# Another order of the query tiles in stick-breaking attention, on Trainium2

## The reference, cut to what matters

```python
z = jnp.einsum('bhqd,bhkd->bhqk', qi, kf).astype(jnp.float32) * scale
qpos = bi * SB_BLOCK + jnp.arange(SB_BLOCK)
before = kpos[None, :] < qpos[:, None]
log_beta = jax.nn.log_sigmoid(z)
log_1m = jnp.where(before, jax.nn.log_sigmoid(-z), 0.0)
tail = lax.cumsum(log_1m, axis=3, reverse=True) - log_1m
w = jnp.where(before, jnp.exp(log_beta + tail), 0.0)
return jnp.einsum('bhqk,bhkd->bhqd', w.astype(vf.dtype), vf)
...
mixed = jnp.concatenate(
    [rms_norm(o_a, ga), rms_norm(o_b, gb), rms_norm(o_c, gc)], axis=-1)
y = jnp.einsum('bse,ed->bsd', mixed, w_out[l])
```

## Time and profile before

| | |
|---|---|
| median of 3 runs | 1045.97 us (1045.08 to 1047.18) |
| profiled execution | 1044.86 us |
| its span | 1043.1 us |
| TensorE busy | 1015.7 us, 97% of the span |
| VectorE, ScalarE, GpSimd busy | 795.8, 572.3, 90.5 us |
| granted TensorE clock, mean | 0.998 |

### The profile page before, as it was taken

One profiled execution on the slowest core, in us unless ns is written; L12 is line 12 of the kernel. 1 busy time (PEld: TensorE's weight loads), 2 busy tenths in 40 slices (PEclk: granted clock), 3 DMA queues, 4 the chain that ended last, 5 costly groups with the idle time before them and its releaser, 6 DMA issues.

```text
span 1043.1 us, 12464 instructions
## 1 busy us (share of the span) xinstructions
PE 1015.7 (97%) x4982; PEld 820.1 (79%) x4982; DVE 795.8 (76%) x740; ACT 572.3 (55%) x753; POOL 90.5 (9%) x71
## 2 busy tenths in 40 slices
PE   8999999998989999999999999999999999999996
PEld 6878778786757787788788888788888788888784
DVE  6247659688578579877878867998776998777998
ACT  6513432658767536677653567333657333666454
POOL 0014113021211143000000000000000000000000
PEclk9999999999999999999999999999999999999999
DMA  9421111200011544013013022022031031035004
GB/s 327 139 76 41 41 41 41 71 11 2 2 41 41 193 165 167 1 42 120 1 47 116 1 76 87 1 79 83 1 121 41 1 121 41 1 123 201 1 0 161
DMA packets 38657, 74.65 MB, mean 72 GB/s; under 512 B 3236, under 2 KB 12744, under 8 KB 38600
## 3 DMA queue, kind: packets, MB, share of 16 engines
q1 hardware_dynamic: 38600, 73.86, 20.5%
HBM read 65.46 MB, written 8.39 MB: 71 GB/s over the span
## 4 chain that ended last, share of the span: by engine, by line
PE 87%; DVE 5%; ACT 4%; issue 1%; DMA 1%; SPq 1%; ACTq 0%; DVEq 0%
PE ps L720 27%; PE ps L724 27%; PE ps L722 26%; PE ps L889 2%; PE ps L935 2%; PE ps L793 1%; PE ps L960 1%; DMA xt<-in_x_turned 1%; ACT work L1158 1%; DVE out_gained L2090 1%; DVE y L2148 1%; DVE y L2039 1%; ACT sb_w L1330 1%; PE ps L824 1%; ACT sb_r L1326 0%
## 5 line engine op out<-in xcount | busy, mean ns | idle before, releaser
L720 PE MATMUL ps<-a_op,b_op 128*128 128x512 f32 x448 | 175.6, 392 | 3.0 <-ACT ut L1435 1.1
L720 PE MATMUL ps<-b_op,a_op 128*128 128x512 f32 x448 | 174.7, 390 | 3.9 <-issue 3.9
L724 PE MATMUL ps<-a_op,b_op 128*128 128x512 f32 x448 | 174.5, 389 | 0.0
L724 PE MATMUL ps<-b_op,a_op 128*128 128x512 f32 x448 | 174.4, 389 | 0.0
L722 PE MATMUL ps<-a_op,b_op 128*128 128x512 f32 x448 | 174.4, 389 | 0.0
L722 PE MATMUL ps<-b_op,a_op 128*128 128x512 f32 x448 | 174.4, 389 | 0.0
L1484 ACT CAST a_op<-f 128x1024 fp32r<-128x1024 f32 x56 | 58.8, 1050 | 113.2 <-PE ps L724 73.0
L720 PE MATMUL ps<-act_hi,w_hi 128*128 128x512 f32 x288 | 114.5, 398 | 2.6 <-issue 1.3
L1996 DVE TENSOR_TENSOR b_op<-wq,b_op 128x1024 fp32r<-128x1024 f32 x96 | 117.0, 1219 | 0.0
L724 PE MATMUL ps<-act_hi,w_lo 128*128 128x512 f32 x288 | 112.2, 390 | 0.0
L722 PE MATMUL ps<-act_lo,w_hi 128*128 128x512 f32 x288 | 112.2, 390 | 0.0
(11 more groups left out here) (224 smaller groups left out, 1682.9 us busy)
## 6 DMA issues: line engine op xcount, KB each, us to landing
wq<-in_w_ff_in SPq DMA_DIRECT2D x16, 1024.0 KB, 5.6
wq<-in_w_ff_out SPq DMA_DIRECT2D x16, 1024.0 KB, 5.2
stage<-in_w_in SPq DMA_DIRECT2D x16, 512.0 KB, 4.8
y<-in_x SPq DMA_DIRECT2D x4, 1024.0 KB, 12.5
stage<-in_w_out SPq DMA_DIRECT2D x8, 512.0 KB, 3.9
h_spill<-y SPq DMA_DIRECT2D x8, 512.0 KB, 2.7
h_back<-h_spill SPq DMA_DIRECT2D x2, 2048.0 KB, 11.9
out<-y SPq DMA_DIRECT2D x8, 512.0 KB, 2.8
```

The lines of the kernel that those rows point to most:

```text
L720: nc.tensor.matmul(dst, stat[0], mov[0], start=first, stop=False, skip_group_check=chained)
L724: return nc.tensor.matmul(dst, stat[1], mov[0], start=False, stop=last, skip_group_check=chained)
```

## The change

The units come in another order: the first pair runs t = 7, 6, 5, 4, 0, 1, 2, 3, the second 4, 5, 6, 7, 3, 2, 1, 0. The fill rows move with them and again leave out the units with one and two key blocks (now u = 4, 5, 14, 15). SUM_UNIT goes from 6 to 4, and with it GpSimd's addition of the window squares (from ahead of the mask of head 10 to ahead of that of head 6), TensorE's partition sums and VectorE's reading of them, which is now tied to head 12. The window group's roundings on ScalarE go from heads 17 and 19 to 9 and 11, their VectorE halves from heads 21 and 23 to 13 and 15. The squares after heads 3 and 5 and the splits after heads 7 and 21 stay. The table load goes from behind head 29's copies to behind the loop.

```diff
--- before.py
+++ after.py
@@ -392,7 +392,9 @@
 
 
 
-        UNITS = [(p, t) for p in range(2) for t in reversed(range(TOK))]
+
+        UNITS = [(p, t) for p, ts in ((0, (7, 6, 5, 4, 0, 1, 2, 3)), (1, (4, 5, 6, 7, 3, 2, 1, 0)))
+                 for t in ts]
         HEADS = 2 * len(UNITS)
         CHAIN = 4
         LEAD = 3
@@ -421,10 +423,11 @@
 
 
         WINDOW_ROWS = 2
-        FILL_UNITS = (0, 1, 2, 3, 4, 5, 8, 9, 10, 11, 12, 13)
+        FILL_UNITS = (0, 1, 2, 3, 6, 7, 8, 9, 10, 11, 12, 13)
         N_EARLY = WINDOW_ROWS + len(FILL_UNITS)
-        SUM_UNIT, SPLIT_HEADS = 6, (7, 21)
-        MIX_HEADS = (17, 19)
+        SUM_UNIT, SPLIT_HEADS = 4, (7, 21)
+        AFTER_SUMS = min(u for u in FILL_UNITS if u > SUM_UNIT)
+        MIX_HEADS = (9, 11)
 
         def row_of(u):
             return WINDOW_ROWS + FILL_UNITS.index(u)
@@ -976,7 +979,7 @@
                     pe.wait_ge(turned_copied, 4)
                 elif n < N_EARLY:
                     pe.wait_ge(row_copied, n)
-                    if n == row_of(FILL_UNITS[6]):
+                    if n == row_of(AFTER_SUMS):
                         pe.wait_ge(grp_var, 2)
                 elif n == N_EARLY:
                     pe.wait_ge(row_copied, N_EARLY)
@@ -1015,7 +1018,7 @@
                 if u in FILL_UNITS:
                     recurrent_out(row_of(u), range(2, OUT_K))
                 if u == SUM_UNIT:
-                    pe.wait_ge(row_copied, row_of(FILL_UNITS[6]))
+                    pe.wait_ge(row_copied, row_of(AFTER_SUMS))
                     group_sums(1, 7, win_sq[:, 0, :])
             weighted(len(UNITS) - 1)
             for n in range(N_EARLY, 2 * TOK):
@@ -1394,8 +1397,7 @@
                     split_hi(N_IN + 1, (N_IN + 1) % 2)
                 if n == SPLIT_HEADS[1]:
                     split_hi(N_IN + 2, N_IN % 2)
-                if n + LEAD == HEADS:
-                    nc.scalar.preload_act_table_set("natural_log_exp_and_others")
+            nc.scalar.preload_act_table_set("natural_log_exp_and_others")
             output_copy(len(UNITS) // CHAIN - 1)
             group_rsqrt(1)
 
@@ -1914,7 +1916,7 @@
                     split_lo(N_IN + 1, (N_IN + 1) % 2)
                 if n == SPLIT_HEADS[1] + 2:
                     split_lo(N_IN + 2, N_IN % 2)
-                if a and u == SUM_UNIT + 1:
+                if n == 2 * SUM_UNIT + 4:
                     group_variance(1, 7)
             left = list(range(N_EARLY, 2 * TOK))
             for k in range(2):
```

## The result

The changed kernel takes 1050.26 us (median of six runs, 1049.93 to 1051.42) against 1045.97 (1045.08 to 1047.18): a ratio of 1.0040, 95% interval 1.0030 to 1.0051. It is slower by 4.3 us, by more than the 0.2% that can be told from no change, and inside the range of 1045.8 to 1050.4, though 2.3 above the forecast of 1048.0. Its profiled execution took 1050.91 us with a span of 1049.2.

The account below looks back on a forecast made before the run. TensorE, computing for 97% of the span, was taken as the bound. Idle time rising from 3.8 to 6.3 us, less 0.45 for the table load, gave +2.0 on the median 1045.97: 1048.0, range 1045.8 to 1050.4.

Parts of the forecast that it names:

- the old handover: Kernel before, 297 to 308 us: smallest unit of first pair to largest of second; 2.81 us TensorE idle, forecast to go.
- Part 1: Window sum ahead of head 6's mask on GpSimd: TensorE idle 4.2 us before head 6's transposes, 4.05 as shown.
- Part 2: Weight split after head 7 beside one-block units: 1.2 us idle at unit 6's scores, replacing 0.75 before.
- Part 3: Roundings beside units 4 and 5 without fill: waits of 0.55 at unit 7's scores, 0.9 at unit 5's weighted sum.
- Part 4: From unit 6 on: heads ready 2 to 6 us early; the waits of 2.81 and 0.21 us go.
- Part 5: Table load behind the loop: TensorE goes on sooner after head 31's copy, gain 0.45 us, bound 0.2 to 0.5.
- The sum: Whole kernel: idle time 3.8 to 6.3 us, less 0.45 at the end: +2.0 us, bounds +0.8 and +3.2.
- The clock falls: Rival: TensorE drops to half clock after the 4.2 us wait; 4 us of work costs 2, total +4, 1050; chance 0.12.
- Handover covered: Rival: the first wait comes but those of parts 2 and 3, 2.75 us, don't: -0.7, 1045.2; chance 0.13.
- VectorE becomes the bound: Rival: four big units in a row make heads 20 to 23 late, 1 to 2 us more, 1049.3; chance 0.09.
- The window sum is not on the path: Rival: head 6's mask does not wait for GpSimd's sum, so -2.2 us, 1043.8, faster; chance 0.08.

Follow-up runs that it names:

- the filled wait: Changed kernel plus 12 extra 512-column matmuls, result unused, between the scores of unit 4 and head 6's transposes: 1049.19 us, ratio 1.0024.
- the old handover kept busy: Kernel before plus 12 extra unused matmuls, six ahead of unit 9's scores and six ahead of head 16's transposes: 1044.88 us, ratio 0.9996.
- The first two experiments: Changed kernel, window sum ahead of head 8's mask: 1044.36 us, ratio 0.9985; kernel before, sum ahead of head 6's mask: 1052.81 us, ratio 1.0056.
- the eighth experiment: The kernel with split and roundings moved, but second pair running t = 7 down to 0: 1041.90 us, ratio 0.9965.
- the kernel with split and roundings moved: Changed kernel, window sum ahead of head 8's mask, first weight split after head 6, window roundings after heads 12 and 14: 1042.38 us, ratio 0.9966.
- changed kernel kept busy twice: Changed kernel plus 12 extra unused matmuls in the wait for head 6's mask and six in loop 4: 1049.23 us, ratio 1.0025.

## Why the prediction was right, and where it was off

**The clock as a cost of every run.** The times of before's runs in all the experiments, by the mean granted clock of the run:

| mean granted clock | runs | mean us |
|---|---|---|
| 0.998 | 20 | 1044.19 |
| 0.997 | 20 | 1046.10 |
| 0.996 | 10 | 1045.62 |
| 0.995 | 8 | 1046.06 |
| 0.994 | 18 | 1047.14 |
| 0.992 | 16 | 1047.75 |

The steps aren't even, but most of the scatter goes with the clock: 0.998 is 3.6 us below 0.992. The changed kernel's six runs all lie at 0.994 and 0.993. The profiled execution of before, at 0.998, had the highest clock of its kind, and I took its clock for the kernel's. Averaged, the kernel before loses some 1.8 us to the clock (its median of 1045.97 against 1044.2) and the changed one some 2.7 to 2.9 (1050.26 against the 1047.4 to 1047.6 above). So the 4.3 us are 3.2 to 3.4 of idle time and about 1 of clock. That each kernel loses time to the clock is shown, by the filled wait and by the old handover kept busy; how the difference divides is an estimate.

**Part 1, the sum ahead of head 6: right.** Predicted start of the sum 277.7, measured 278.06, of which 0.35 is the offset of the whole trace. Predicted wait as shown 4.05, measured 3.95. The first two experiments show its cause from both sides. What the step left out is what follows the wait: 3.4 us at half clock. Loop 3 took 7.97 instead of 6.33, +1.64, and the filled wait gave 1.6 of it back.

**Part 2, the split beside small units: right.** Predicted 1.2 us (1.1 as shown) at the scores of unit 6, measured 1.17, and with the split one head earlier (and the roundings moved) 0.2 was left. The clock fell some 3 us behind it.

**Part 3, the roundings beside units without fill: sizes off.** Predicted waits as shown 0.4 and 0.75, measured 0.1 and 0.53. TensorE ran at half clock from 295.1 on, so it is likely that it reached these points later and found ScalarE ready. The time wasn't saved: from head 8's transposes at 289.60 to head 11's at 298.28 it took 8.7 where my steps gave 7.8 (287.7 to 293.8, 0.55 of waiting and 1.13 for the scores of unit 7).

**Part 4, from unit 6 on: wrong.** I said that each head would be ready 2 to 6 us early and no wait would come. Heads are early, but TensorE also needs a PSUM bank for its transposes, and ScalarE's copies free it. These stand behind the sigmoids of a unit that has grown. In the changed kernel at head 18:

```profile
316.37 0.92 ACT L1329 ACTIVATE sb_r<-ps 128x896 f32<-128x896 f32 x1 [1.65 <-PE ps L938]
317.19 0.91 ACT L1333 ACTIVATE sb_w<-ps 128x896 f32<-128x896 f32 x1
317.98 0.76 ACT L1345 COPY work<-ps 128x512 f32<-128x512 f32 x2
```

Two sigmoids of 896 columns precede the copy, and TensorE's transposes, next at 318.72, wait 0.32 for it; at 326.94 it is 0.43. Loops 8 and 9 took 7.41 and 8.22, and these two waits of 0.75, with 0.15 of drain in front of each, make about 1.05 of that. The trace of before had shown the same thing, in the old handover, and I passed it over:

```profile
307.65 0.66 PE L889 MATMUL ps<-ident,sb_w 128*128 128x128 f32 x4 [1.28 <-ACT work L1342]
```

The second half of head 16's transposes waited there for the copy of head 15's (307.33), behind two sigmoids of 896 columns (305.72 and 306.53). The part went wrong at this step: it priced TensorE's wait for a copy at nothing. Following only the path of data and not that of the buffers was the fault. Descending units, in the eighth experiment, don't have these waits. The rest of the part held: the 2.81 us of the old handover are gone, and no wait on VectorE came near 325 to 340.

**Part 5, the table load: right in the trace.** From head 26's transposes to the row product behind the loops it took 351.13 - 341.71 = 9.42 before and 357.09 - 348.09 = 9.00 after: a gain of 0.42, predicted 0.45. The load takes 1.28 us at 356.69, and ScalarE's next instruction starts at 357.98, 1.29 behind it. No drain shows, as I had assumed from the earlier trace rows, against the 1.38 us of the Trainium skill (ScalarE: Activation LUTs, What ACT_TABLE_LOAD costs). In the medians it can't be told from the clock's scatter.

**The sum.** To head 24's transposes I had +1.8 (the 2.5 of idle time less the 0.65 of work that moved behind this point) and the trace shows +5.4. Of the 3.6 between them, 1.6 is loop 3's clock, 0.9 loops 4 and 5, 1.1 the bank waits, less 0.2 for the shorter wait of part 3; some 0.2 I can't place. In the tail the two terms, +0.65 and -0.4, are as reckoned. The measured median is still only 2.3 above my forecast, and that is luck: the steps were short by 3.6 us in this stage, or 4.0 over the whole execution, and 1.8 of that (6.05 against 4.3) disappears only because the two profiled executions lie on opposite sides of their medians. Two terms that I put at nothing failed, the clock behind the first wait (1.6) and the bank waits (about 1.1).

**The rivals.** *The clock falls* was the one that came about on top of the forecast. Its price, 4 us at half clock for 2, had no row behind it; each of the changed kernel's two falls lasted 3.4 us, and the first cost 1.6. I gave it 0.12 because the wait of 4.2 was shorter than the 4.6 us after which the clock fell at the end of the span, and because it stayed up through 297 to 308. Both were single observations: the traces show the fall right after a wait of 3.95 and of 4.29, and behind a stretch of 4.6 us with 3.48 busy (the kernel before with the table load moved). The Trainium skill (TensorE: Matmul & The Clock Gate, Part 1: The HAM clock gate) says the gate opens by activity and is closed by default. The traces agree in so far as the clock stood at half behind the waits of 3.95 and 4.29 and at full level again 3.4 us later, and I should have weighed this more than one undisturbed execution. *Handover covered* fell with the measured 1.17; the waits that it priced at 2.75 sum to 2.65 in parts 2 and 3 (1.2, 0.55, 0.9), or 2.25 as the stretch table shows them, which I used in the sum. *VectorE becomes the bound*: no such wait. *The window sum is not on the path*: it is, by both experiments.

## What to carry to other kernels

When tiles are reordered, follow every instruction that is placed by head or unit number on its own in-order queue: here one GpSimd sum, one mask too early, turned a change worth some 0.15% (0.34% with split and roundings placed well) into a loss of 0.40%. Follow buffers as well as data, look in the trace before the change for waits of the kind that you price at nothing, and price an idle stretch of TensorE with the clock behind it. Before trusting one profiled execution as the baseline, look at the mean granted clock of the other runs.

## What the runs showed of the hardware

- The clock fell in stretches where the page shows TensorE as busy: in the kernel with split and roundings moved it was busy for 3.66 of 3.70 us, with 35 matmuls, 16 of them of one column, and then ran at 0.54 for 3.4 us. A busy share near 1 doesn't show that the clock will hold.
- The falls lasted about 3.4 us (changed kernel, 281.5 to 284.9), 6.8 (changed kernel kept busy twice, 294.4 to 301.2) or 10.2 to 10.3 (old order with the sum ahead of head 6's mask, 308.3 to 318.5; wait filled, 292.0 to 302.3).
- The same kernel scatters from 1043.8 to 1048.3 us, and most of this follows the mean granted clock. An edit worth 0.4 us (the table load) can be read in a trace and not in a median.
- A mask of 128 by 128 on GpSimd takes 0.29 us alone and up to 1.87 in this stage of the changed kernel (at 329.55), beside a VectorE scan of 1023 columns that runs from 329.05 to 331.33.
